# Modulation matrices spread over the attention stretch, the input in quarters, and the first tokens' fetched rows in front of the last expert's rows

## What is computed

```python
def reference(x, ..., c_2, ctx_2, c_ctx_2, ada_w_2, ada_b_2, ...):
    x = first_block(x, ...)      # attention (fox), a recurrence (rg_lru), sparse attention (nsa), gating
    return second_block(x, c_2, ctx_2, c_ctx_2, ada_w_2, ada_b_2, ...)

def first_block(...):
    z = rms_norm(x, norm_g) @ w_in            # qa ka va ... mg, split by columns
    y_a = fox_attention(...); y_b = rg_lru(...); y_c = nsa_attention(...); y_d = spatial_gating(...)
    ...                                        # each times silu of its gate, then the "merge"
    merged = sum(sigmoid(mg) * (ys @ w_branch), over the four branches)
    return x + merged @ w_out

def second_block(x, c, ctx, c_ctx, ada_w, ada_b, ...):
    mod_x, mod_c = ada_modulation(c, ...), ada_modulation(c_ctx, ...)   # silu(cond) @ ada_w + ada_b, 1024 x 6144
    ...                                        # norms scaled and shifted by mod_x, mod_c; mixers
    ff_x = moe_ffn(hx2, router_w, router_b, moe_w_gate, moe_w_up, moe_w_down)   # 16 experts
    return rmsnorm(x + mod_x[5] * ff_x, final_norm_g)
```

## Time and profile before

| | |
|---|---|
| median of three timed runs | 1151.13 us |
| the profiled execution's own time | 1146.38 us |
| its span | 1144.6 us |
| PE busy | 1022.7 us (89%) |
| DVE busy | 588.6 us (51%) |
| ACT busy | 409.6 us (36%) |
| DMA | 230.64 MB, 202 GB/s on average |
| mean granted TensorE clock | 0.942 of full |

### The profile page before, as it was taken

The page is one execution under the profiler, slowest core; times in us unless marked ns, Lnnn a source line. Parts: engine busy times, 40 slices in busy tenths (PEclk is TensorE's granted clock), DMA queues, the critical chain, the costliest instruction groups (busy, mean ns, idle before and its releaser), DMA issues.

```text
span 1144.6 us, 13539 instructions
## 1 busy us (share of the span) xinstructions
PE 1022.7 (89%) x5502; PEld 751.9 (66%) x5502; DVE 588.6 (51%) x1043; ACT 409.6 (36%) x678; POOL 48.2 (4%) x66
## 2 busy tenths in 40 slices
PE   5989898698888799998997999999598999999974
PEld 3464787466447698895986788689585663375531
DVE  2272512765434456431646579874773431387815
ACT  2212433645215455221446410142662310276501
POOL 1000000000000000000001022200000000000010
PEclk9999899699888899999998999999699999999988
DMA  9623264024993529334422314400497999899994
GB/s 311 199 74 110 74 221 147 1 74 150 383 391 110 193 96 327 148 127 173 156 74 96 111 41 147 145 1 1 155 408 259 385 338 379 306 406 405 408 366 165
DMA packets 110348, 230.64 MB, mean 202 GB/s; under 512 B 8236, under 2 KB 15693, under 8 KB 110286
## 3 DMA queue, kind: packets, MB, share of 16 engines
q1 hardware_dynamic: 104080, 216.44, 52.2%
q0 software_dynamic: 2880, 9.71, 2.2%
q10 hardware_dynamic: 3326, 3.63, 1.0%
HBM read 221.11 MB, written 8.65 MB: 201 GB/s over the span
## 4 chain that ended last, share of the span: by engine, by line
PE 71%; DVE 14%; DMA 8%; ACT 4%; issue 2%; ACTq 0%; DVEq 0%; SPq 0%
PE bank L650 11%; PE bank L620 9%; PE bank L2456 6%; PE bank L1393 5%; PE bank L1395 5%; PE bank L1394 5%; PE bank L2395 4%; PE bank L2396 4%; PE bank L2397 4%; DMA slot<-in_ada_w 3%; PE bank L2480 3%; DMA more_slots<-in_moe_w_up 2%; DMA slot<-in_w_in 2%; PE bank L2388 2%; PE bank L1436 2%
## 5 line engine op out<-in xcount | busy, mean ns | idle before, releaser
L1393 PE MATMUL bank<-rounded 128*128 128x256 f32 x560 | 165.5, 296 | 4.8 <-DVE slot_rounded L1383 4.2
L1394 PE MATMUL bank<-rounded 128*128 128x256 f32 x560 | 158.8, 284 | 0.0
L650 PE MATMUL bank<-x_and_h,slot 128*128 128x256 f32 x608 | 142.2, 392 | 4.9 <-ACT x_and_h L548 4.9
L650 PEld LDWEIGHTS bank<-x_and_h,slot 128*128 128x128 f32 x608 | 117.7, 197 | 22.9 <-issue 6.4
L1395 PE MATMUL bank<-rounded,slot_rounded 128*128 128x256 f32 x440 | 125.3, 285 | 0.0
L1393 PEld LDWEIGHTS bank<-rounded 128*128 128x128 f32 x560 | 107.6, 192 | 12.0 <-issue 8.1
L1394 PEld LDWEIGHTS bank<-rounded 128*128 128x128 f32 x560 | 107.5, 192 | 1.3 <-issue 1.0
L1383 DVE TENSOR_TENSOR slot_rounded<-slot,rounded 128x1024 fp32r<-128x1024 f32 (+1 forms) x63 | 67.8, 1097 | 71.4 <-ACT rounded L1377 71.2
L620 PE MATMUL bank<-slot,x_and_h 128*128 128x512 f32 x224 | 99.3, 601 | 4.5 <-DVE x_and_h L585 4.5
L1395 PEld LDWEIGHTS bank<-rounded,slot_rounded 128*128 128x128 f32 x440 | 84.6, 192 | 0.0
L620 PEld LDWEIGHTS bank<-slot,x_and_h 128*128 128x128 f32 x224 | 42.8, 193 | 56.0 <-issue 55.1
(11 more groups left out here) (484 smaller groups left out, 1990.1 us busy)
## 6 DMA issues: line engine op xcount, KB each, us to landing
slot<-in_w_in SPq DMA_DIRECT2D x27, 2048.0 KB, 8.6
slot<-in_ada_w SPq DMA_DIRECT2D x12, 2048.0 KB, 12.7
slot<-in_moe_w_down SPq DMA_DIRECT2D x11, 2048.0 KB, 16.6
more_slots<-in_moe_w_gate SPq DMA_DIRECT2D x8, 2048.0 KB, 15.5
more_slots<-in_moe_w_up SPq DMA_DIRECT2D x8, 2048.0 KB, 18.4
slot<-in_moe_w_gate SPq DMA_DIRECT2D x7, 2048.0 KB, 10.1
x_and_h<-in_moe_w_up SPq DMA_DIRECT2D x6, 2048.0 KB, 15.8
more_slots<-in_moe_w_down SPq DMA_DIRECT2D x5, 2048.0 KB, 17.4
```

Source lines behind the costliest of these rows:

```text
L650: mm = t.do.matmul(bank[:, 0:S], w[:, k, i * P:(i + 1) * P], h[:, k, :], start=k == 0, stop=k == KT - 1)
L1393: t.do.matmul(dst, w_hi, x_hi, start=start, stop=False)
L1394: t.do.matmul(dst, w_hi, x_lo, start=False, stop=False)
```

## The change

Four things change:

1. `ada`'s 24 jobs are taken from behind `spatial` and spread evenly over `early + lru + spatial`, from the 11th of these jobs on (`spread`). The zeroed home of the condition vectors (`cond_wide`) moves to words that are free from the start, and POOL clears it at the start. `h1_split` still stands in front of `("ada", 6)` and moves with it.
2. `xT` is fetched by four DMAs of 256 KB instead of one of 1 MB, and ACT squares two tiles as each lands. The first piece of weights comes in two halves.
3. PE does 20 matmuls of 128 columns on the matrix of ones in front of the first norm's sums. Their result is overwritten.
4. In the tail, DVE adds the first 128 tokens' fetched rows (`rows_picked(0)`) in front of the last block's `rows`; the other half's stand behind the first half's banks.

```diff
+def spread(main, extra, first):
+    out, n = list(main[:first]), 0
+    for i, job in enumerate(main[first:]):
+        out.append(job)
+        while n * (len(main) - first) < (i + 1) * len(extra):
+            out.append(extra[n])
+            n += 1
+    return out
...
-        fill, scored = early + lru + spatial + ada + merge[1], attention(UNITS)
+        fill, scored = spread(early + lru + spatial, ada, 10) + merge[1], attention(UNITS)
...
-        cond_wide = v_tm[:, 0, 0:32 * KT].rearrange("p (k n) -> p k n", k=KT)
+        cond_wide = arena[:, KEPT:KEPT + 32 * KT].rearrange("p (k n) -> p k n", k=KT)
...
+            g.do.memset(cond_wide, 0.0).then_inc(*inc("cond_clear"))      # gpsimd_constants
...
             for k in range(KT):
+                if tag == "h1":
+                    a.wait_ge(*at(f"x{k // 2}_in"))
...
+            if tag == "h1":
+                for _ in range(N_WARM):                                    # N_WARM = 20
+                    t.do.matmul(bank[:, 0:P], ones[:, :], ones[:, :], start=True, stop=True)
...
-            s.do.dma_start(xT[:, :, :], d["xT"].rearrange("(k p) s -> p k s", p=P)).then_inc(*dma("x_in"))
+            for i in range(4):
+                x = slice(2 * i, 2 * i + 2)
+                s.do.dma_start(xT[:, x, :], d["xT"].rearrange("(k p) s -> p k s", p=P)[:, x, :]).then_inc(*dma(f"x{i}_in"))
...
+            def rows_picked(tt):
+                v.wait_ge(*at("residual_back"))
                 for which in range(2):
                     v.wait_ge(*at(f"picked{tt}{which}_in"))
                     v.do.scalar_tensor_tensor(out=x_tok[:, tt, :], in0=picked[which][:, tt, :], scalar=share[:, which, tt:tt + 1], in1=x_tok[:, tt, :],
                                               op0=ALU.mult, op1=ALU.add).then_inc(*inc("x3", "picked", tt, which))
                     v.wait_ge(*now("x3"))
...
             for job in EXPERT_JOBS:
+                if job == ("rows", len(BLOCKS) - 1):
+                    rows_picked(0)
                 if job[0] in steps:
                     steps[job[0]](*job[1:])
             for tt in range(NT):
+                if tt:
+                    rows_picked(tt)
                 for half in range(2):
```

More of the change, by code:

```diff
@@ L64 @@
 HIGH_RING = 4
+N_WARM = 20
 KEPT = ARENA - 2 * S
@@ L77 @@
     TOPICS = ("cmp", "hg", "hy", "fourier", "ctx", "filter", "taps", "response", "norm2", "norm", "lru", "spatial", "final", "router",
-              "decay", "forget", "softplus", "shares", "combine", "head", "heads", "keys", "gates", "ada", "row", "cat", "moe", "split")
+              "decay", "forget", "softplus", "shares", "combine", "head", "heads", "keys", "gates", "ada", "row", "cat", "moe", "split", "x", "y")
     def __init__(self, nc, ctx, counted):
@@ L530, in scalar_norm_squares @@
             src, src_done, dst, gain, mod, squares = NORMS[tag]
-            if tag == "h1":
-                a.wait_ge(*at("x_in"))
             if tag == "hc":
@@ L616, in tensor_tokens @@
             bank, w = psum.take(t, ("tokens", name, tt)), loads_view[name]
-            t.wait_ge(*loaded(name))
+            t.wait_ge(*(at("first_half_loaded") if name == LOADS[0] else loaded(name)))
             for k in range(KT):
+                if name == LOADS[0] and k == KT // 2:
+                    t.wait_ge(*loaded(name))
                 t.wait_ge(*at(h_done, k))
@@ L1284, in build @@
         cond = par_of("cond", 0, 16).rearrange("p (k c) -> p k c", c=2)
-        @part(GPSIMD, "ada")
-        def gpsimd_ada(g, c):
-            if c == 0:
-                g.wait_ge(*at("mixed", ("fox", WT - 1, NT - 1)))
-                g.do.memset(cond_wide, 0.0).then_inc(*inc("cond_clear"))
         @part(SCALAR, "ada")
@@ L2806, in rows @@
                                            ALU.mult).then_inc(*inc("moe_rows_v", b, half))
-            steps = {"split_tokens": split_tokens, "split": split, "gated": gated, "turn": turned, "rows": rows}
-            for job in EXPERT_JOBS:
-                if job[0] in steps:
-                    steps[job[0]](*job[1:])
-            v.wait_ge(*at("residual_back"))
-            for tt in range(NT):
+            def rows_picked(tt):
+                v.wait_ge(*at("residual_back"))
                 for which in range(2):
@@ L2819, in vector_experts @@
                     v.wait_ge(*now("x3"))
+            steps = {"split_tokens": split_tokens, "split": split, "gated": gated, "turn": turned, "rows": rows}
+            for job in EXPERT_JOBS:
+                if job == ("rows", len(BLOCKS) - 1):
+                    rows_picked(0)
+                if job[0] in steps:
+                    steps[job[0]](*job[1:])
             for tt in range(NT):
+                if tt:
+                    rows_picked(tt)
                 for half in range(2):
@@ L2824, in vector_experts @@
                     v.do.tensor_tensor(x, x, psum.of["added", tt, half][:, :], ALU.add).then_inc(*inc("x3", *((tt,) if half else ("first", tt))))
-                v.wait_ge(*now("x3"))
             v.wait_ge(*at("final_row_in"))
@@ L2883, in sync_program @@
                     s.wait_ge(*at(*SLOT_FREE_AFTER[name]))
-                s.do.dma_start(loads_view[name], WEIGHTS[name][0]).then_inc(*dma(f"slot{SLOT_OF[name]}_loaded", name))
+                first = 0
+                if n == 0:
+                    first = KT // 2
+                    s.do.dma_start(loads_view[name][:, 0:first, :], WEIGHTS[name][0][:, 0:first, :]).then_inc(*dma("first_half_loaded"))
+                s.do.dma_start(loads_view[name][:, first:, :], WEIGHTS[name][0][:, first:, :]).then_inc(*dma(f"slot{SLOT_OF[name]}_loaded", name))
             sync_experts(s)
```

## The result

The changed kernel takes 1133.75 us (median of 4 runs, 1128.37 to 1137.38) beside 1150.99 us for the kernel before (4 runs, 1148.79 to 1152.27): ratio 0.9848, 95% interval 0.9805 to 0.9892, so 17 us faster with 12 to 22 possible. The forecast was 1122.5 us, 28.6 us faster. The result lies inside the range of 1110 to 1136 and outside the likeliest one, 1115 to 1129: only the reach towards the rivals takes it in. 40% of the expected gain is missing, and by the prediction's own mark (a merge that starts less than 20 us earlier) something in it is wrong. Another 6 runs later gave 1134.30 us and 0.9860 (0.9835 to 0.9884).

What follows compares the result with a forecast made beforehand. PE's waits and half clock bound it, through DMA at the modulation, DVE and ACT at the recurrence. -26.5 - 2.3 - 1.9 - 1.0 + 3 + 1.5 - 2.0 + 0.6 = -28.6 us: 1151.1 to 1122.5, likeliest 1115 to 1129, 8 in 10 1110 to 1136.

Steps and rivals of the forecast that it cites:

- The modulation, taken out of its stretch: From 278.1 to 347.9 us, PE's waiting and half clock around the modulation go: 26.5 us gained.
- The merge's gate at full clock: First merge's gate: weights fetched further ahead, so PE comes to it without a stop; 2.3 us gained.
- Where it lands: Moved jobs partly fill PE's waits for DVE at `keys` (1.9 us) and before `cmp_turn` (1.0 us).
- The recurrence: Between first convolution and last step, DVE gets added work; PE loses 13 us as before, plus 3 us.
- Takes half of it: Rival: PE can't run ahead in the recurrence, 13 us lost instead of 3, 4 more around; 1136 us, chance 0.17.
- gaps are filled: Rival: added jobs take the waits at `flip`, clock stays high; gain 38 to 41 us, 1112 us, chance 0.20.
- Late loads: Weight pieces fetched just in time, tightest at `ada` 3 and `gb`: 1.5 us lost, bounds 0 and 6.
- The rival: Loads come late: four or five of 12 pieces, 12 us lost, gain of 18, 1133 us; chance 0.08.
- the recurrence's rival: PE can't run ahead there: 13 us lost instead of 3, 4 more around; gain 15 us, 1136 us, chance 0.17.
- The start: First norm's sums end at 11.2 us instead of 12.9, by warming matmuls and quartered input: 2.0 us gained.
- The bound of a gain of 4.9 us: Upper bound at the start: all 20 warming matmuls at full clock, then the input decides.
- The tail: DVE starts the last rows 0.6 us later, for the residual, without waiting for PE's last matmuls: 0.6 us lost.

Runs made afterwards that it cites:

- e7: e4 with the first merge's rounding and splitting (ACT and DVE) two jobs earlier, in front of the third spatial step: 1128.68 us, ratio 0.9812.
- e4: The changed kernel with the conditioning vector's silu on ACT right behind the first norm's root: 1129.26 us, ratio 0.9814.
- e8: e4 without the recurrence's four reciprocals on DVE, which its result needs: 1124.89 us, ratio 0.9782.
- e6: e4 with 14 of the 24 modulation jobs ahead of the recurrence, 10 behind it and none inside: 1122.92 us, ratio 0.9765.
- e5: e4 with the recurrence's steps in turns with the projections ud and vd: 1117.34 us, ratio 0.9696.
- e2: The kernel before with only the input in quarters, 20 warming matmuls and the halved first load: 1149.45 us, ratio 0.9992.
- e9: e4 with e5's order, the old tail, 14 modulation jobs ahead of the recurrence and 10 behind its gates: 1111.70 us, ratio 0.9673.
- e10: e4 with 20 more matmuls on the ones in PE's wait for DVE ahead of the first projection: 1126.63 us, ratio 0.9783.
- e3: The kernel before with only the new tail order, two fetched rows in front of the last expert's rows: 1151.39 us, ratio 1.0010.

## Why the prediction fell short, step by step

- **The modulation, taken out of its stretch, -26.5: right.** From the first scan to the gate 19.0 us idle and 7.4 by the clock went to nothing, 26.4 in all.
- **The merge's gate at full clock, -2.3: the step held, the size did not.** 0.5 came; PE's wait of 1.57 us for DVE's split took most of the rest. The prediction asked what would be late next for the weights, and not for DVE. e7 moved the split and gained nothing.
- **Where it lands, -1.9 - 1.0: the step that failed.** The prediction wrote that the first `ada` "fills 1.9 of them" and gave it no wait of its own. It put ACT's two more table loads into ACT's idle time and did not ask where in ACT's order the silu stands that `ada` waits for, though before's trace has the 3.22 us of that wait at the old place. `cmp_turn` gained 1.6 us, as against 1.0. In all the stretch lost 3.1 us instead of gaining 2.9. e4 undoes the silu's place alone and gets back 4 to 5 us.
- **The recurrence, +3: right in kind, +4.8 in size.** 14.6 us lost before, 19.4 after. e8 shows that DVE's work is on the path there, e6 that the added jobs cost more than they fill, e5 that PE with projections beside it loses half as much. "Takes half of it" (13 us and more) was too much, "gaps are filled" had the wrong sign.
- **Late loads, +1.5:** 0.4 us of waiting. The rival gave nearly the time that was measured, 1133, by a mechanism that did not occur; that is chance. So is the nearness of the recurrence's rival, 1136: it wanted 13 us there.
- **The start, -2.0: mis-sized.** Earned 1.87 us at the first projection; e2 measured 0.9, with nothing possible. What was said of the half clock behind it, that it would stay, failed: in the changed kernel's profile it grew from 3.4 to 6.9 us. In e9 it was 3.4 us and the projection took 29.40 us as before, but the warming itself took 7.22 us instead of 6.25; the projection's end, 46.26 and 45.90 us against 46.80, is little earlier either way. e10 shows the gap behind the sums to be the cause. The bound of a gain of 4.9 us doesn't follow from its terms: 1.3 + 20 x 0.22 + 3.5 us is 9.2, a gain of 3.7.
- **The tail, +0.6: the wait for the residual right, the rest not.** 1.6 us were lost in the changed kernel, 0.3 in e3. The step that failed is that DVE "doesn't wait for PE's last matmuls": it waited 0.86 and 0.61 us for them, at the half clock. e3's time (0.3 us faster to 2.5 slower) agrees but doesn't show it alone.

From the gates to the merge: -26.4 + 3.1 + 4.8 = -18.5, and 1.9 us more of PE's own work at full clock (176.0 and 177.9 us), is -16.7 with rounding; the traces have -16.8. I can't assign these 1.9 us to an instruction, but they go with where the modulation's jobs stand: PE's own work is 177.8 us in e4 and e5 as well, and 176.4 and 176.3 in e6 and e9, which have 14 of the 24 jobs ahead of the recurrence. Against the forecast's 28.6 us the first stretch has 4.5 (+3.1 where -1.4 was counted with the loads), the recurrence and the gate 1.8 each, the start 1 to 2, the tail 1.0, and the unassigned work 1.9: 12 or 13 us, where 11.4 are missing by the medians and 6 to 16 by the interval.

## What to carry to other kernels

When a job is moved, go through what each of its waits needs on every engine, small instructions too: an activation of 16 columns that cost 3.2 us in the old place cost 8.4 in the new one, for what stood ahead of it on ACT, and nothing at all once it was issued early. Where one engine sets the pace of a stretch, filling another engine's gaps with jobs that need the first one as well makes it longer; give it work that needs none of it (e5, two lines of order, was worth 12 to 14 us). And lay single profiles beside each other only for places: two of the same order stood 4 us apart here. A piece that hardly shows in the time can be seen from one common place to the end, over several traces: so the new tail's 1.6 us came out.

## What the runs showed of the hardware that I had not expected

- A wait of 4.5 us of PE, right behind 5 to 11 us of matmuls, was accompanied in every kernel without a bridge by 3.4 or 6.9 us at 1.2 GHz, which began within it or less than 1 us behind. With the wait filled by matmuls on ones (e10), the clock stayed at 2.4 GHz until 64 us into the execution, where PE's next wait for DVE stands, and the projection took 27.70 us instead of 29.40 or 30.73.
- Warming alone moved the lower level rather than removed it. Where the clock rose between 4.2 and 4.6 us (the changed kernel twice, e2, e7) the fall at the wait took 6.9 us, and where it rose between 6.1 and 7.5 us (e4, e5, e8, e9) it took 3.4; the first projection ended between 45.7 and 46.3 us in all eight. In e6 it rose at 5.0 us, fell for 3.4 with 0.5 of them inside the wait, and the projection ended at 44.9 us, 1.9 us ahead of before. So what warming earned changed from one execution to the next.
- Four DMAs of 256 KB, issued one behind the other, had a median of 4.2 us to landing, and the first squares ran at 4.08 us; one of 1 MB took 5.6. They ran beside each other: one behind the other, four times 4.2 us would be 16.8, and ACT had squared the last of them at 7.87.
- An ACT table load took 1.28 us and the silu began 1.30 us behind its start.
